# The second block's gates as six pairs of seven half products, with the sums of h made beside the first tiles

## What is computed

```
xn = rms(x) * gain;   proj = xn @ w_in                      # 1024 x 6152 columns
o_a = gated delta rule(q, k, v, g, beta)                    # 4 heads of 128
o_a = rms(o_a) * dn_out_gain * silu(z_a);  y_a = o_a @ w_up_a
o_b = stick_breaking(q_b, k_b, v_b) * silu(z_b);  y_b = o_b @ w_up_b
gates = sigmoid(proj[..., last 2048] + b_gate)              # 2 x 1024 columns
merged = gates[..., :1024] * y_a + gates[..., 1024:] * y_b
x = x + merged @ w_out
```

## Time and profile before

| | us |
|---|---|
| median of 3 runs | 3000.65 (2998.07 to 3002.27) |
| the profiled execution, its own time | 3002.73 |
| its span | 3001.0 |
| TensorE busy | 2872.9 (96%) |
| VectorE busy | 1465.0 (49%) |
| GpSimd busy | 1094.7 (36%) |
| ScalarE busy | 909.6 (30%) |
| mean granted TensorE clock | 0.989 |

### The profile page before, as it was taken

One profiled execution on the slowest core, in us unless ns is written; L12 is line 12 of the kernel. 1 busy time (PEld: TensorE's weight loads), 2 busy tenths in 40 slices (PEclk: granted clock), 3 DMA queues, 4 the chain that ended last, 5 costly groups with the idle time before them and its releaser, 6 DMA issues. The chain is left out here.

```text
span 3001.0 us, 48110 instructions
## 1 busy us (share of the span) xinstructions
PE 2872.9 (96%) x20106; PEld 2296.8 (77%) x20106; DVE 1465.0 (49%) x1675; ACT 909.6 (30%) x1364; POOL 1094.7 (36%) x749
## 2 busy tenths in 40 slices
PE   7999788999999999999999999999999899989999
PEld 6777677778878876788888888777877777866677
DVE  6554442432465434533333333777578433357561
ACT  5433222231011123422222222433333332357410
POOL 1331212444345430344444544211211444435552
PEclk9999999999999999999999999999999999999999
DMA  5333333433142111111111111022324534321143
GB/s 209 85 126 112 100 90 80 134 116 91 28 144 66 49 49 42 36 43 57 57 57 56 50 57 50 22 77 72 98 92 113 170 89 134 112 88 64 60 140 126
DMA packets 308553, 258.29 MB, mean 86 GB/s; under 512 B 46754, under 2 KB 269145, under 8 KB 308362
## 3 DMA queue, kind: packets, MB, share of 16 engines
q1 hardware_dynamic: 308106, 255.47, 28.0%
q10 hardware_dynamic: 256, 0.07, 0.0%
HBM read 191.79 MB, written 63.31 MB: 85 GB/s over the span
## 5 line engine op out<-in xcount | busy, mean ns | idle before, releaser
L280 PE MATMUL ps<-h_hi,w_hi 128*128 128x512 f32 x1584 | 511.5, 404 | 6.5 <-POOL w_lo L177 3.7
L280 PE MATMUL ps<-h_lo,w_hi 128*128 128x512 f32 x1584 | 490.5, 391 | 0.0
L280 PE MATMUL ps<-h_hi,w_lo 128*128 128x512 f32 x1584 | 489.2, 390 | 0.0
L161 POOL TENSOR_TENSOR w_hi<-w_raw,ones 128x1024 fp32r<-128x1024 f32 x90 | 218.7, 2429 | 570.4 <-PE ps L280 393.9
L280 PEld LDWEIGHTS ps<-h_hi,w_hi 128*128 128x128 f32 x1584 | 295.9, 188 | 97.5 <-issue 34.4
L280 PEld LDWEIGHTS ps<-h_hi,w_lo 128*128 128x128 f32 x1584 | 298.5, 188 | 63.5
L280 PEld LDWEIGHTS ps<-h_lo,w_hi 128*128 128x128 f32 x1584 | 298.1, 188 | 63.6
L818 POOL TENSOR_TENSOR op_lo<-w_raw,op_hi 128x512 fp32r<-128x512 f32 x160 | 206.2, 1294 | 371.1 <-ACT op_hi L807 370.5
L164 POOL TENSOR_TENSOR w_lo<-w_raw,w_hi 128x1024 fp32r<-128x1024 f32 x90 | 233.0, 2589 | 7.1
L1367 DVE TENSOR_TENSOR x_t<-x_t,ps 128x512 f32<-128x512 f32 x128 | 87.7, 687 | 223.2 <-PE ps L859 207.3
L177 POOL TENSOR_TENSOR w_lo<-w_raw,w_hi 128x1024 fp32r<-128x1024 f32 x30 | 74.2, 2473 | 303.8 <-ACT w_hi L172 303.8
(11 more groups left out here) (573 smaller groups left out, 5442.4 us busy)
## 6 DMA issues: line engine op xcount, KB each, us to landing
w_raw<-in_w_in_dram SPq DMA_DIRECT2D x91, 512.0 KB, 4.7
w_raw<-in_w_up_dram SPq DMA_DIRECT2D x32, 512.0 KB, 4.1
w_raw<-in_w_down_dram SPq DMA_DIRECT2D x32, 512.0 KB, 3.4
kv_raw<-in_w_kv_dram SPq DMA_DIRECT2D x16, 512.0 KB, 5.9
mix_gates<-mix_sig SPq DMA_DIRECT2D x16, 512.0 KB, 3.0
mix_gate_b<-mix_gates SPq DMA_DIRECT2D x32, 256.0 KB, 4.0
mix_gates<-w_raw SPq DMA_DIRECT2D x16, 512.0 KB, 2.8
x_in<-in_x_dram SPq DMA_DIRECT2D x8, 512.0 KB, 8.8
```

What stands on the lines that cost most here:

```text
L161: pool.tensor_tensor(c.w_hi[:, s], c.w_raw[:, s], c.ones[:].unsqueeze(1).broadcast_to([P, KT, P]), ALU.mult).then_inc(c.w_rounded, 1)
L280: last = pe.matmul(o, w[:, s, k], a[:, k - offset, (half + h) * width:(half + h + 1) * width], start=(k == kts[0] and w is c.w_hi and a is ...
```

## The change

A new function `pair_gates` takes the place of `gates` for the second block.

- Tiles 0 to 3 stay whole: tile 0 in the delta rule as before, 1 to 3 in the stage.
- The other 12 tiles are six pairs of seven half products (class `PairStream`, built on `MlpStream`), without the MLP's other work between them.
- Four sums of quarters of h are made in the meantime (class `HalfSums`), in four parts j each: sum 1 on GpSimd (three instructions and the rest), sums 3, 2 and 4 on VectorE in PSUM (3, 2 and 2 instructions, then three rests), all rounded by ScalarE. They lie where x and the unused half of the branch buffers are.
- The side step (0, 0) comes with tile 2, (0, 1) and (1, 0) with pair 0, then one with each pair. Its matmul has bank 5 instead of 4, but for the first.
- Results leave in four quarters per pair, each with its own eviction, Sigmoid and store of 128 x 512.
- Weight tiles use two slots, shifted by one.
- q, k and v of stick-breaking are loaded one by one inside the last pair, and TensorE's wait for the mask moves behind the transposes.
- In `gates` the branches for `late` go away; the first block's use of it is the same.

The core of the diff, the queues of `pair_gates` (`s` is the stream, `t` the sums, `side` the side step; `o = s.PAIR_OPS * p`, `where = lambda p: (1 + p // 2, p % 2)`):

```
+            @block.sync
...
+                for p in range(n_pairs):
+                    s.fetch(sp, 2 * p + 3)
+                    side.load(sp, *where(p))
+                    store_quarter(p, 0)
+                    s.fetch(sp, 2 * p + 4)
+                    if p == n_pairs - 1:
+                        following(sp, s, t)
+                    for m in (1, 2, 3):
+                        store_quarter(p, m)
...
+            @block.gpsimd
+            def _(pool):
+                t.pool_form(pool, 0)
+                t.pool_form(pool, 1)
+                weights.split_tile(pool, 0, 2)
+                t.pool_split(pool, 0)
+                t.pool_split(pool, 1)
+                t.pool_form(pool, 2)
+                weights.split_tile(pool, 0, 3)
+                t.pool_form(pool, 3)
+                t.pool_split(pool, 2)
+                t.pool_split(pool, 3)
+                weights.done(pool, 0, 2)
+                for p in range(n_pairs):
+                    s.pool_products(pool, p)
...
+                    pe.wait_ge(freed, 4 * p + 1 if p else 3)
+                    s.product(pe, o, ps[:, A], *b11).then_inc(s.used, 1)
+                    if p:
+                        pe.wait_ge(freed, 4 * p + 2)
+                    s.product(pe, o + 1, ps[:, E], *t.at(1), before=after_split(1)).then_inc(s.used, 1)
+                    if p == 0:
+                        pe.wait_ge(t.split[3], HK)
+                        side.pe_after(pe, 0, 1)
+                    pe.wait_ge(xcopied, 3 * p + 1)
+                    s.product(pe, o + 2, ps[:, B], *t.at(2), start=False, before=after_split(2)).then_inc(s.used, 1)
+                    if p:
+                        side.pe_after(pe, *where(p))
+                    s.product(pe, o + 3, ps[:, A], *b21, start=False).then_inc(s.used, 1)
+                    pe.wait_ge(xadded, 2 * p + 1)
+                    s.product(pe, o + 4, ps[:, B], *t.at(3), start=False, before=after_split(3)).then_inc(s.used, 1)
+                    if p == 0:
+                        side.pe_after(pe, *where(p))
+                    s.product(pe, o + 5, ps[:, C], *b22, start=False).then_inc(s.used, 1)
+                    pe.wait_ge(xcopied, 3 * p + 3)
+                    s.product(pe, o + 6, ps[:, DD], *t.at(4), start=False, before=after_split(4)).then_inc(s.used, 1)
...
+                for p in range(n_pairs):
+                    o = s.PAIR_OPS * p
+                    seed_u(p)
+                    s.round(act, o + 4)
+                    keep_fifth(p)
+                    if p == 0:
+                        side.act_after(act, 0, 1)
+                    else:
+                        side.act_before(act, *where(p))
+                    s.round(act, o + 5)
+                    s.round(act, o + 6)
+                    if p == 0:
+                        side.act_late(act, 0, 1)
+                        side.act_before(act, *where(p))
+                    else:
+                        side.act_after(act, *where(p))
+                    s.round(act, o + 7)
+                    gate_quarter(p, 0)
+                    seed_last(p)
+                    s.round(act, o + 8)
+                    if p == 0:
+                        side.act_after(act, *where(p))
+                    else:
+                        side.act_late(act, *where(p))
+                    gate_quarter(p, 1)
+                    s.round(act, o + 9)
+                    gate_quarter(p, 2)
...
+                    s.round(act, o + 10)
+                    gate_quarter(p, 3)
...
+                sums(0)
+                dve.wait_ge(factor_loaded, 16)
+                evict(0)
+                sums(1)
+                side.dve(dve, 0, 0)
+                evict(1)
+                sums(2)
+                evict(2)
+                sums(3)
+                evict(3)
+                side.dve(dve, 0, 1)
+                for p in range(n_pairs):
+                    add_fifth(p)
+                    take(p, 0)
+                    if p:
+                        side.dve(dve, *where(p))
+                    end_fifth(p)
+                    take(p, 1)
+                    take(p, 2)
+                    if p == 0:
+                        side.dve(dve, *where(p))
+                    take(p, 3)
```

More of the change, by code:

```diff
@@ L2626, in gates, with build @@
     out = scratch(c, f"{name}_gates", [2, KT, P, SEQ])
-    def build(side, sig, after=None, late=None, following=lambda sp, weights: None):
+    def build(side, sig, after):
         weights.begin()
[L2630 to L2635, removed]
+        after.weights.begin()
         gated = c.sem(f"{name}_gated")
@@ L2659, in turn @@
                             store(i - 1, per - 1)
-                        if last and after and u:
+                        if last and u:
                             if u > 1:
@@ L2678, in _ @@
                 turn(weights.turns - 1, last=True)
-                following(sp, weights)
                 store(weights.turns - 1, per - 1)
[L2681 to L2687, removed]
+                after.load(sp)
+                for n in range(len(sig)):
+                    sp.wait_ge(stored[n], 16 * weights.turns * share)
             @block.gpsimd
@@ L2691, in _ @@
                 weights.split(pool)
-                if after:
-                    after.weights.split(pool)
-                    after.following.split_first(pool)
+                after.weights.split(pool)
+                after.following.split_first(pool)
             @block.tensor
@@ L2711, in turn @@
                         weights.ready(pe, i, u)
-                        wait(pe, freed if late else gated, i * per + (u - 1))
+                        wait(pe, gated, i * per + (u - 1))
                         b = 2 * (u % 2)
@@ L4817, in __init__, with load_one, load_first @@
         self.loaded = [c.sem(f"sb_loaded{q}") for q in range(2)]
+    def load_one(self, sp, ct, n):
+        sp.dma_start(self.tile[ct % 2][n][:], self.src[n][ct]).then_inc(self.loaded[ct % 2], 16)
     def load(self, sp, ct):
         for n in "qkv":
-            sp.dma_start(self.tile[ct % 2][n][:], self.src[n][ct]).then_inc(self.loaded[ct % 2], 16)
-    def load_first(self, sp, weights):
-        sp.wait_ge(self.c.tile_done, weights.t0 + weights.total - 1)
-        sp.wait_ge(self.c.w_split, weights.t0 + weights.total)
-        self.load(sp, 0)
+            self.load_one(sp, ct, n)
+    def load_first(self, sp, stream, sums):
+        sp.wait_ge(sums.split[1], HK)
+        self.load_one(sp, 0, "k")
+        sp.wait_ge(stream.pooled, stream.released(2 * stream.pairs - 3))
+        self.load_one(sp, 0, "v")
+        sp.wait_ge(stream.used, stream.total - 3)
+        self.load_one(sp, 0, "q")
 def stick_breaking(c, following, inputs):
@@ L4978, in _ @@
                 turn_values(0, h)
+            pe.wait_ge(made, 2)
             score(0)
```

316 lines of the change are left out of this document (283 added, 33 removed).

## The result

The changed kernel takes **3037.5 us** (median of 4 runs, 3035.1 to 3038.2), the kernel before 3000.4 (4 runs, 2998.1 to 3002.3): ratio 1.0123, 95% interval 1.0105 to 1.0140. It is slower by 37 us, as forecast (3035, range 3009 to 3051). The profiled execution took 3038.01 us, 35.3 more than the 3002.73 of the profiled one before. The total was hit, but terms of the sum were wrong in size and cancelled: the waits together with the port were put too high, the clock too low.

The account below looks back on a forecast made before the run. TensorE was taken to bound the gate stage: 154.7 us work, 46.2 stalls and restarts make 202 against 172.4, +29.6; stage end -3.0, port +5, clock +4 and -1 give +34.6, less 2.1: 3035 us, range 3009 to 3051.

Parts of the forecast that it names:

- the port: Side steps: VectorE instructions with two SBUF inputs wait for GpSimd's instruction to end; +5 us, bounds 0 and +11.
- the clock: Behind TensorE's five stalls of 5.3 to 7.1 us the granted clock may fall; 0.8 us each, +4.
- Removed products: Second block's gate stage: twelve tiles become six pairs of seven products, 72 matmuls less, 16.4 us.
- The stage's end: After the gate stage's last matmul, TensorE's idle time falls from 5.64 to 2.7 us; gain 3.0.
- The loads: Pairs: do_o and do_z queue behind a weight fetch awaiting GpSimd's SUM5, so TensorE's normalising matmul stalls 5.0 us.
- The late ScalarE: Pairs 1 to 4: half Sigmoids waiting for VectorE delay ScalarE's seed copy, adding 1.1 us to the stall.
- The start: Gate stage's first tiles and pairs: four queues laid out in written order give TensorE stalls, among them 5.3 and 4.8 us.
- Tile 3 and product 4: TensorE waits on VectorE: 5.3 us before tile 3, 4.8 us before product 4 of pair 0.
- Rival B: Gate stage: clock falls at each long stall, costing 4 us each instead of 0.8; 3051 us, chance 0.13.
- the -1: Behind the gate stage's end, the shorter idle gap may keep the clock up: 0 to -3.5 us, taken as -1.
- 154.7: TensorE's work in us in the new gate stage if nothing stalls it: whole tiles, pairs and normalising matmuls.
- 46.2: Sum in us of TensorE's forecast stalls in the gate stage, 25.4 of them in pairs 1 to 4.

Follow-up runs that it names:

- experiment 7: The reordered kernel with twelve more matmuls that nobody reads behind each pair's seventh product: 3002.2 us, ratio 0.9997.
- Experiment 1: Changed kernel with SyncE's do_o and do_z loads issued ahead of the weight fetch in pairs 1 to 5: 3009.9 us, ratio 1.0021.
- Experiment 8: Changed kernel with the side step's reciprocal written to PSUM, so VectorE's product of o has one PSUM operand: 3026.9 us, ratio 1.0082.
- experiment 10: The reordered kernel with all three products of the side step kept in PSUM: 2985.7 us, ratio 0.9939.
- Experiment 2: Changed kernel with 24 unread matmuls added before the normalising matmul in each of pairs 1 to 4: 3028.6 us, ratio 1.0079.
- experiment 9: Changed kernel with all three VectorE products of the side step kept in PSUM: 3028.6 us, ratio 1.0078.
- experiment 3: Changed kernel, VectorE reordered at the start: eviction 1 before side step (0, 0), pair 0's addition before side step (0, 1): 3037.3 us, ratio 1.0122.
- experiment 5: Changed kernel with side loads ahead of the weight fetch and the normalising matmul after product 4 instead of 2: 3016.1 us, ratio 1.0044.
- the reordered kernel: Changed kernel with the same instructions, but the queue orders of SyncE, ScalarE, VectorE, GpSimd and TensorE rewritten: 2988.5 us, ratio 0.9955.

## Why the prediction was right, and where it was not

**Removed products, right.** -16.4; experiment 7 measured 2.72 us per product, and 13.7 in the time, which counts five of the six.

**The stage's end, right.** 2.7 us idle were planned and 2.91 measured; the gain is 2.7 where 3.0 stood.

**The loads: the right chain, 1 us too short.** From the end of product 0 to the normalising matmul I planned 10.5 us plus 1.1 for a late ScalarE, 11.6. In the pair shown it is 12.6 (2610.48 to 2623.12): 6.3 to the fetch's issue, 5.6 from there to the Square, 0.7 to the matmul. But TensorE too came later, 6.2 us after product 0 instead of 5.46 (0.29 of it a wait for the late seed), so its wait is 6.45 where I had 6.1. The waits of pairs 1 to 4 come to 26.1 us (planned 25.4). Experiment 1 shows that the fetch ahead is the cause: without it the load is issued earlier, and from do_o's issue (2573.77) to the Square (2577.72) it takes 3.95 us instead of 5.14. I had taken 5.81 from the fetch's issue with a load ahead, here 5.64, and 3.83 without one; both are borne out.

**The late ScalarE and the port, right in mechanism, too small.** ScalarE's seed copy starts 2.55 us after product 0 in the pair shown, and 0.19 after it in the MLP's: 2.4 late, planned 1.1. I had costed the half Sigmoids' waits for VectorE (19.8 us over 11 times) with VectorE's products at their undisturbed length, and put the port aside as +5. Experiment 8 shows how the two hang together: with one product off the port the seed starts 1.10 us after product 0 in pairs 2 to 4, 0.9 late, close to my 1.1. The port's part comes on top of it and goes on to GpSimd's sum and the fetch. It is worth some 10 us of the stage (210.7 to 200.5), where I took 5: TensorE's waits are 7.9 us shorter (40.6 to 32.7) and its busy time 2.3 (170.1 to 167.9). So most of it stands inside the waits that I had planned.

**The start, too dear.** Planned were 18.5 us of waits up to product 2 of pair 1; measured are 0.88, 5.26, 5.33 and 0.70, 12.2. Tile 3 and product 4 are right to half a microsecond. The steps that failed are the 2.8 for products 0 to 2 of pair 0 and the 2.7 of its normalising matmul, which did not come, and product 2 of pair 1, 0.7 instead of 2.2. For the normalising matmul the trace shows why: do_o was issued at 2536.22 with no fetch ahead, its Square began at 2539.44, and TensorE was inside product 4, which the low clock (0.70 over 2536.5 to 2544) stretched to 4.8 us, until 2541.59. At 2.73 us it would have ended some 0.6 us before the Square did, so even then the wait would have been short.

**The clock, the mis-sized term.** I took 0.8 us for each of five waits, +4; there were six waits over 5 us, and the layout had put the sixth, before product 4, at 4.8. Working backwards: stage 210.7, less waits 40.6, less the work with its restarts 155.9, leaves 14.2 us. (The 155.9 is borne out by experiment 10, 155.8 us busy at clock 1.00.) The rows say where it lies. Behind the four long waits TensorE is busy 22.5, 23.3, 22.1 and 22.8 us for 86 matmuls, and 20.5 in experiment 1 at clock 1.00: 8.7 us more. Experiment 2 gives nearly the same by another way, 8.4. Product 4 of pair 0 took 4.8 us instead of 2.73, 2.1 more, and behind the wait before tile 3 the clock is 0.83 over 2504 to 2514, by estimate 1.5 us. That makes 12.3, or 2 us for each of the six waits. The last 2 us lie in matmuls at the full clock, where I had taken 0.1 for each restart; their cause isn't shown. I had argued from the light work in the earlier trace rows that a full stream would recover more cheaply; it did not. The Trainium skill's advice (TensorE: Matmul & The Clock Gate, Why this matters for your kernels) against gaps of some microseconds between bursts, which I had weighed against my +4, was right here: every wait over 5 us in this stage had low clock in the matmuls behind it. How long it lasted did not follow the wait: 23.3 us busy behind 6.18 us idle, 22.1 behind 6.45. Rival B's mechanism held, at about half its price. Nor did the shorter gap at the stage's end save the -1: the clock is 0.51 over 2691 to 2699, where the earlier trace rows have 0.50.

So the sum of the stage was 154.7 (its parts give 154.5) + 46.2 + 1.2 + 5 + 4 = 211.1, measured 210.7, by 155.9 for work, 40.6 for waits (the port's part inside) and 14.2 for the clock. Waits 10.6 too long with the port counted, clock and restarts 10.2 too short: that they cancelled is luck, and 3035 against 3037.5 is better than the terms deserve.

What stays open: what sets how long the low clock lasts behind a wait, and with it why experiment 9 gained nothing over experiment 8; and which moves of the reordering count.

## What to carry to other kernels

When less work is asked of the bounding engine, the order in which the other queues serve it has to be laid out again as a whole: here a load behind one fetch that waits for another engine cost 28 us, more than the 16 that the products saved, and moving single items elsewhere only moved the wait (experiment 3) or took back part of the gain (experiment 5). In this kernel a wait of 6 us on TensorE had to be priced at 8, since the clock falls behind it. An operand in PSUM takes a VectorE instruction out of GpSimd's way: that gave 10.6 us where VectorE stood in the chain that feeds TensorE, and nothing clear of the noise in the reordered kernel, where 5 us of waits were left in all.

## What the runs showed of the hardware

Adding 96 matmuls whose result nobody reads made the kernel 9 us faster (3028.6 against 3037.5), since the granted clock stayed at 1.00 through the pairs. After the wait of 6.18 us the matmuls started 0.43 us apart, after the one of 1.50 us in experiment 1 they started 0.23 apart. Getting one VectorE instruction off the shared port shortened the next one too, from 1.43 to 0.97 us, though its operands had not changed; the third went from 0.72 to 0.84.
